# A state space layer scanned over 128 chunk states of four tokens instead of over 512 tokens

## The reference, cut to what matters

```python
bu_re = jnp.einsum('blgh,gph->blgp', uf, bbar_re)     # and bu_im
a_re = jnp.broadcast_to(ar, (1, L, SSM_GROUPS, SSM_STATE))   # ar, ai: the same at every token
_, _, xr, xi = lax.associative_scan(_s5_combine, (a_re, a_im, bu_re, bu_im), axis=1)
y = (jnp.einsum('blgp,ghp->blgh', xr, c_re) - jnp.einsum('blgp,ghp->blgh', xi, c_im) + d * uf)
y = jax.nn.gelu(y)
z = y @ w_glu + b_glu                                  # gated output of the mixer
```

## Time and profile before

| | |
|---|---|
| median of three runs | 2510.85 us (2506.82 to 2512.15) |
| the profiled execution | 2511.58 us, its span 2509.8 us |
| TensorE matmul busy | 2283.3 us (91% of the span) |
| VectorE busy | 1359.9 us (54%) |
| mean granted TensorE clock | 0.95 |
| last chunk of the mixer taken by VectorE (L1526) | starts at 249.98 us of the span |

### The profile page before, as it was taken

One profiled execution on the slowest core, in us unless ns is written; L12 is line 12 of the kernel. 1 busy time (PEld: TensorE's weight loads), 2 busy tenths in 40 slices (PEclk: granted clock), 3 DMA queues, 4 the chain that ended last, 5 costly groups with the idle time before them and its releaser, 6 DMA issues.

```text
span 2509.8 us, 28343 instructions
## 1 busy us (share of the span) xinstructions
PE 2283.3 (91%) x10166; PEld 1763.3 (70%) x10166; DVE 1359.9 (54%) x1988; ACT 924.8 (37%) x1334; POOL 263.4 (10%) x217
## 2 busy tenths in 40 slices
PE   5777888999998899999998789999979978999997
PEld 3511556788886688888887658888857865888885
DVE  7998555544445556665655454234258874532433
ACT  5400332322222555655554143123144432422322
POOL 4477003000004000000000100000100001000000
PEclk9898888999999999999999899999999988999999
DMA  3000011222322212212221212222211111222221
GB/s 147 32 0 0 26 67 67 84 92 92 103 79 103 86 66 81 80 63 80 69 74 55 68 67 91 93 101 100 77 50 68 58 51 67 100 87 98 101 91 43
DMA packets 32218, 185.50 MB, mean 74 GB/s; under 512 B 4753, under 2 KB 5009, under 8 KB 13457
## 3 DMA queue, kind: packets, MB, share of 16 engines
q1 hardware_dynamic: 27216, 176.17, 20.0%
q10 hardware_dynamic: 2880, 6.20, 0.7%
q0 software_dynamic: 2048, 2.17, 0.4%
HBM read 180.26 MB, written 2.10 MB: 73 GB/s over the span
## 4 chain that ended last, share of the span: by engine, by line
PE 74%; DVE 10%; issue 5%; ACT 5%; DVEq 4%; POOL 3%; ACTq 0%; DMA 0%; POOLq 0%
PE ps L516 14%; PE ps L518 14%; PE ps L517 14%; PE ps L833 5%; PE ps L835 5%; PE ps L834 5%; POOL prod L456 2%; PE ps L573 2%; PE ps L539 1%; PE ps L541 1%; PE ps L540 1%; DVE f_run L1937 1%; PE ps L652 1%; DVE rstd L1358 1%; ACT h L1253 1%
## 5 line engine op out<-in xcount | busy, mean ns | idle before, releaser
L516 PE MATMUL ps<-x_hi,w_lo 128*128 128x512 f32 x1024 | 403.6, 394 | 24.0 <-DVE u L1513 12.0
L517 PE MATMUL ps<-x_lo,w_hi 128*128 128x512 f32 x1024 | 401.9, 392 | 0.0
L518 PE MATMUL ps<-x_hi,w_hi 128*128 128x512 f32 x1024 | 401.7, 392 | 0.0
L970 ACT ACTIVATE w_hi<-raw 128x2048 fp32r<-128x2048 f32 x122 | 233.0, 1910 | 423.4 <-PE ps L518 362.7
L1346 DVE TENSOR_TENSOR w_lo<-raw,w_hi 128x2048 fp32r<-128x2048 f32 x122 | 284.5, 2332 | 97.0 <-ACT w_hi L970 96.7
L516 PEld LDWEIGHTS ps<-x_hi,w_lo 128*128 128x128 f32 x1024 | 194.5, 190 | 70.0 <-DVE w_lo L1346 25.1
L516 PE MATMUL ps<-hid_hi,w_lo 128*128 128x512 f32 x602 | 234.2, 389 | 0.0
L517 PE MATMUL ps<-hid_lo,w_hi 128*128 128x512 f32 x602 | 234.2, 389 | 0.0
L518 PE MATMUL ps<-hid_hi,w_hi 128*128 128x512 f32 x602 | 234.2, 389 | 0.0
L833 PE MATMUL ps<-x_hi,w_lo 128*128 128x512 f32 x560 | 229.1, 409 | 4.8 <-DVE w_lo L1819 4.8
L518 PEld LDWEIGHTS ps<-x_hi,w_hi 128*128 128x128 f32 x1024 | 194.2, 190 | 40.9
(11 more groups left out here) (344 smaller groups left out, 3619.2 us busy)
## 6 DMA issues: line engine op xcount, KB each, us to landing
raw<-w_attn_in SPq DMA_DIRECT2D x32, 1024.0 KB, 4.8
raw<-w_gate_up SPq DMA_DIRECT2D x22, 1024.0 KB, 4.8
raw<-w_up_a SPq DMA_DIRECT2D x16, 1024.0 KB, 4.8
raw<-w_down_a SPq DMA_DIRECT2D x16, 1024.0 KB, 4.8
raw<-w_up_h SPq DMA_DIRECT2D x16, 1024.0 KB, 4.8
raw<-w_down_h SPq DMA_DIRECT2D x16, 1024.0 KB, 4.8
raw<-w_hgrn_in SPq DMA_DIRECT2D x8, 1024.0 KB, 4.7
raw<-w_down SPq DMA_DIRECT2D x8, 768.0 KB, 4.2
```

Source lines behind the costliest of these rows:

```text
L516: pe.matmul(o, w_lo[:, slot, a:a + P], hi[:, k, :], start=k == 0, stop=False)
L517: pe.matmul(o, w_hi[:, slot, a:a + P], lo[:, k, :], start=False, stop=False)
L518: last = pe.matmul(o, w_hi[:, slot, a:a + P], hi[:, k, :], start=False, stop=k == st.kc - 1)
L970: act.activation(w_hi[:, slot, :], raw[:, slot, :], ACT.Copy).then_inc(whi_ready, 1)
```

## The change

With four tokens to a chunk (`STEP`), the state need only be known at the chunk's start. What the tokens of a chunk do to each other goes through a direct matrix of 128x128 for each of the distances 0 to 3 (`k_tau`), and what they add to the state at the chunk's end is summed by TensorE over the four phases (`ssm_in` with `lw`, which holds B times a power of a). Turning and scanning then run over 128 chunk states (`CHUNKS`) for each pair, in two batches of eight pairs, and the output of a token is C times a power of a (`ca_re`, `ca_im`) times the state before its chunk. u is stored by phase (`by_phase`), so that each phase's 128 tokens are contiguous.

New or altered on each engine: VectorE does the reciprocal and the first two tiles before the angles, does the angles of all pairs in seven 128x2048 instructions, and builds powers of a, `ab_re`/`ab_neg` and `ca_re`/`ca_im`. TensorE makes 32 transposes in place of 8 and 128 matmuls of 32x32 for `k_tau`, after the third slab. ScalarE copies eight banks to `lw` and four blocks to `k_tau`, and makes sine and cosine in three 128x2048 instructions. GpSimd only clears buffers. The turning back moves from GpSimd to VectorE. One of ScalarE's start DMAs is gone (B and C come compact in `bc_in`, C also padded as before), and `iota_in` is a quarter of its size.

```diff
+STEP = 4
+CHUNKS = T // STEP
+BATCHES = 2
...
-            for pr in range(N_PAIR):
-                for n, (part, by) in enumerate(((0, cos_t), (0, sin_t), (1, sin_t), (1, cos_t))):
-                    pool.wait_ge(scan_ready, 2 * pr + part + 1)
-                    if pr:
-                        pool.wait_ge(yssm_done, 4 * pr + n - 3)
-                    pool.tensor_tensor(prod[:, n, :], scan[pr % 2][part], by[:, pr, :], ALU.mult).then_inc(prod_ready, 1)
+            for pads in (ab_re, ab_neg, ca_re, ca_im):
+                last = pool.memset(pads[:, :, :, :], 0.0)
+            last.then_inc(pads_zero, 1)
...
+            def input_weights():
+                pe.wait_ge(ab_ready, 1)
+                for j in range(STEP):
+                    for n, ab in enumerate((ab_re, ab_neg)):
+                        if j:
+                            pe.wait_ge(lw_ready, 2 * j + n - 1)
+                        for i in range(4):
+                            last = pe.transpose(ps[:, 2 + n, i * P:(i + 1) * P], ab[:, j, 4 * i:4 * i + 4, :].rearrange("p a c -> p (a c)"), ident)
+                        last.then_inc(lw_done, 1)
+                for i in range(4):
+                    for tau in range(STEP):
+                        for ab, cc in ((ab_re, c_re), (ab_neg, c_im)):
+                            for q in range(4):
+                                at_ = GW * (STEP * i + tau)
+                                last = pe.matmul(ps[GW * q:GW * q + GW, 6, at_:at_ + GW], ab[:, tau, 4 * i + q, :],
+                                                 cc[:, 4 * i + q, :], start=cc is c_re, stop=cc is c_im)
+                last.then_inc(kt_done, 1)
...
+            def ssm_in(bt):
+                if bt:
+                    pe.wait_ge(bu_free, bt)
+                for ii in range(2):
+                    i = 2 * bt + ii
+                    for n in range(2):
+                        for l in range(STEP):
+                            for q in range(4):
+                                rows, at_ = slice(GW * q, GW * q + GW), 2 * P * n + P * ii
+                                last = pe.matmul(ps[:, 2 + q, at_:at_ + P], lw[rows, n, l, i, :], u[rows, i, l, :],
+                                                 start=l == 0, stop=l == STEP - 1)
                 last.then_inc(bu_done, 1)
...
+            def ssm_out(i):
+                for l in range(STEP):
+                    for ca, v in ((ca_re, v_re), (ca_im, v_im)):
+                        for q in range(4):
+                            last = pe.matmul(ps[GW * q:GW * q + GW, (6, SUM)[i % 2], P * l + 1:P * l + P],
+                                             ca[:, l, 4 * i + q, :], v[:, 4 * i + q, 0:CHUNKS - 1], start=False,
+                                             stop=l == STEP - 1 and ca is ca_im, skip_group_check=True)
+                last.then_inc(yssm_done, 1)
...
+            pe.wait_ge(ca_ready, 1)
+            for bt in range(BATCHES):
+                pe.wait_ge(v_ready, bt + 1)
+                for ii in range(2):
+                    if bt:
+                        ssm_direct(2 * bt + ii)
+                    ssm_out(2 * bt + ii)
...
+            def take(t):
+                dve.wait_ge(tile_done, t + 1)
...
             for c in range(5):
-                if c:
-                    split_lo(st, c, 0)
...
                 if c == 1:
+                    split_lo(st, 1, 0)
+                take(2 * c)
+                take(2 * c + 1)
+                if c in (1, 2, 3):
+                    split_lo(st, c + 1, 0)
+                if c == 0:
+                    angles()
+                if c == 1:
+                    input_powers()
                     input_matrix()
...
+                if c == 3:
+                    output_matrix()
...
             modulate(0)
...
+            demodulate(0)
+            modulate(1)
+            demodulate(1)
+            ssm_chunk(0)
+            ssm_chunk(1)
```

More of the change, by code:

```diff
@@ L593, in _ @@
                 if c == 2:
[L594 to L608 removed]
+                    input_weights()
@@ L609, in ssm_in, with ssm_direct @@
                 last.then_inc(bu_done, 1)
-            def ssm_out(pr):
-                i, q = divmod(pr, 4)
-                if q == 0 and i >= 2:
+            def ssm_direct(i):
+                if i >= 2:
                     pe.wait_ge(pre_gelu, i - 1)
-                for n, cc in enumerate((c_re, c_im, c_neg, c_im)):
-                    pe.wait_ge(prod_ready, 4 * pr + n + 1)
-                    pe.matmul(ps[GW * q:GW * q + GW, (6, SUM)[i % 2], :], cc[:, pr, :], prod[:, n, :],
-                              start=n == 0, stop=n == 3).then_inc(yssm_done, 1)
@@ L620, in _ @@
-            pe.wait_ge(blhs_ready, 1)
+                for tau in range(STEP):
+                    pe.matmul(ps[:, (6, SUM)[i % 2], P * tau:T], k_tau[:, i, tau, :],
+                              u[:, i, 0:STEP - tau, :].rearrange("p l c -> p (l c)"), start=tau == 0, stop=False,
+                              skip_group_check=True)
+            def ssm_out(i):
[6 more added lines that the diff above has]
+                last.then_inc(yssm_done, 1)
@@ L621, in _ @@
+            pe.wait_ge(lw_ready, 2 * STEP)
             pe.wait_ge(tile_free["dve"], STAGES["w_in"].tiles)
             ssm_in(0)
+            pe.wait_ge(kt_ready, 1)
+            pe.wait_ge(root_ready, SK["pre_mix"] + 1)
+            ssm_direct(0)
+            ssm_direct(1)
             ssm_in(1)
-            for pr in range(N_PAIR):
-                if pr + 2 < N_PAIR:
-                    ssm_in(pr + 2)
-                ssm_out(pr)
+            pe.wait_ge(ca_ready, 1)
[5 more added lines that the diff above has]
+                    ssm_out(2 * bt + ii)
@@ new lines, in by_power, with each_power, input_matrix @@
+            def by_power(table):
+                return table.unsqueeze(3).to_broadcast([P, STEP, N_PAIR, 16])
+            def each_power(n):
+                return bc[:, n, :, :].unsqueeze(1).to_broadcast([P, STEP, N_PAIR, 16])
+            def input_matrix():
+                g_re, g_im = by_power(gin[:, 0]), by_power(gin[:, 1])
+                for n, (by, src) in enumerate(((g_re, 2), (g_im, 3), (g_re, 3), (g_im, 2))):
+                    tt(ab_part[:, n], by, each_power(src), ALU.mult)
+                settle()
+                dve.wait_ge(pads_zero, 1)
+                for g in range(2):
+                    rows, cols = slice(64 * g, 64 * g + 64), slice(16 * g, 16 * g + 16)
+                    tt(ab_re[rows, :, :, cols], ab_part[rows, 0], ab_part[rows, 1], ALU.subtract)
+                    last = stt(ab_neg[rows, :, :, cols], ab_part[rows, 2], -1.0, ab_part[rows, 3], ALU.mult, ALU.subtract)
+                settle()
+                dve.sem_inc(ab_ready, 1)
@@ new lines, in angles @@
+            def angles():
+                steps = iota[:, :].unsqueeze(1).to_broadcast([P, N_PAIR, CHUNKS])
+                r_hi, r_lo, r_turn = (col(n).unsqueeze(2).to_broadcast([P, N_PAIR, CHUNKS]) for n in ("r_hi", "r_lo", "r_turn"))
+                ang, k, low = sin_c[:, :, :], cos_c[:, :, :], ang_low[:, :, :]
+                tt(k, steps, r_turn, ALU.mult)
+                tt(ang, steps, r_hi, ALU.mult)
+                settle()
+                ts(k, k, ROUND, None, ALU.add)
+                tt(low, steps, r_lo, ALU.mult)
+                settle()
+                stt(k, k, ROUND, ang, ALU.subtract, ALU.subtract)
+                settle()
+                tt(ang, low, k, ALU.subtract)
+                settle()
+                ts(ang, ang, 0.5, -0.5, ALU.min, ALU.max).then_inc(angle_ready, 1)
+                settle()
```

300 lines of the change are left out of this document (158 added, 142 removed).

## The result

The changed kernel takes 2432.0 us, the median of four runs (2428.5 to 2436.4), where the kernel before takes 2511.5. The ratio is 0.9688, with a 95% interval of 0.9667 to 0.9709. The profiled execution took 2430.4 us.

What follows compares the result with a forecast made beforehand. TensorE bounds the whole, but VectorE's scan, GpSimd's products and TensorE's reading bound the mixer loop. Terms summed to the last chunk ending at 197.3 instead of 249.98 us, saving 52.7: 2511.58 to 2458.9, forecast 2459, range 2440 to 2490.

Steps and rivals of the forecast that it cites:

- to the start of `ssm_in`: After TensorE's fourth slab: rounding 1.9, VectorE's rest 2.2, `output_matrix` 9.2 and the last two tiles 1.3 us.
- tail: End of the mixer: two `ssm_direct` 4.2 us, two `ssm_out` 13.7 us, and 2.5 us for the clock.
- I count nothing for that: GpSimd's work shrinks to five clearings, freeing VectorE of slow instructions; no gain was included in the sum.
- I take the serial 0.107: 13.7 us: Two `ssm_out` of 64 passes in the tail: no overlap on four column groups, 0.107 us a pass, 13.7 us.
- I take 0.05: 256 32-column `k_tau` passes at 0.05 us each, 12.8 us (ends 7 and 28); the same price for `ssm_in`, 6.4 us.
- Both signs by which the prediction was to show itself wrong first: `k_tau` passes taking 0.1 us or more, or a 1024-column VectorE instruction taking 2 us.
- The tail's direct products: Two `ssm_direct` on the path at the mixer's end, 4.2 us, plus 2.5 us for the clock after TensorE's idling.
- After the last chunk nothing of the program changes: Code behind the mixer's last chunk is unchanged, so the gain equals how much sooner that chunk ends: 52.7 us.
- The first, everything small overlaps: `k_tau` and `ssm_in` at 0.025 us a pass, `ssm_out` at 2.38 times: 17.5 us less, 2441 us; chance 0.15.
- The second (half clock, no overlap): TensorE's short bursts stay at half clock; `k_tau` and `ssm_in` at 0.107 us, tail doubled: 2494 us; chance 0.10.
- The third: VectorE's instructions with 16-element runs and tiles taken in steps of four tokens cost double: 21.6 us more, 2481; chance 0.13.
- The fourth: Slower than before: each pass pays load and stream in turn at half clock, 0.213 us; 2550 us; chance 0.04.

Runs made afterwards that it cites:

- the run by groups: The changed kernel with the column group as outermost loop of `ssm_out`, so 16 passes in a row go to the same 32 output rows; one run took 2437.4 us.
- the run with sixteen filling products: The changed kernel with sixteen unread 512-column products on TensorE before its wait for the second batch's turned states; the profiled execution took 2427.68 us.

## Why the prediction was wrong

The walk, with my marks and those of the profile after:

| step | forecast, us | measured, us | difference |
|---|---|---|---|
| input's matrices ready | at 78.9 | at 78.6 | -0.3 |
| transposes and copies | 7.0 | 6.3 | -0.7 |
| `k_tau`, 256 passes | 12.8 | 5.0 | -7.8 |
| fourth slab | 11.0 | 12.3 | +1.3 |
| to the start of `ssm_in` | 14.8 | 15.6 | +0.8 |
| first `ssm_in` | 8.9 | 6.4 | -2.5 |
| VectorE's two batches and a chunk | 40.75 | 40.4 | -0.4 |
| tail | 20.4 | 11.6 | -8.8 |
| hand-offs | 2.7 | in the rows above | -2.7 |

Together 21.1 us, which is 197.3 less 176.2.

**What was right.** The bound and its place: the mixer's stretch was set by VectorE and by products on GpSimd, and the change is worth the distance of the last chunk. VectorE's work behind `ssm_in` came out within 0.4 us over 40, and the angles at 14.0 us (42.33 to 56.35) where 13.8 had been forecast. The chunks, which write with a step of 16 bytes, take 1.12 us instead of 0.75. A scan of 128 columns takes 0.40 us and starts each 0.32, where I had 0.37. The fourth slab is longer because it did not find the clock that I gave it: from 89 to 104 us it was 0.89.

**What came out right by luck.** The matrices were ready within 0.3 us of the forecast by errors that cancel. The takes cost 2.0 to 2.1 us a pair and not 1.3, and `input_matrix` 9.9 us and not 9.2; against that the takes began at 40.3 us instead of 42.2 and `input_powers` took 5.9 instead of 6.7. When the same kernel is run again, the takes begin at 42.4 us and the matrices are ready at 80.7. One term was put at nothing ("I count nothing for that"): GpSimd's absence beside VectorE. The seven instructions that end with this one make the rotary angles in both kernels, and took from 33.5 to 39.7 us with GpSimd's angles beside them, which began at 33.8, and from 32.7 to 36.7 us without. Their last, before and now:

```profile
38.39 1.36 DVE L1445 TENSOR_SCALAR tmp<-tmp 128x512 f32<-128x512 f32 x1
36.35 0.43 DVE L1466 TENSOR_SCALAR tmp<-tmp 128x512 f32<-128x512 f32 x1
```

No run removes GpSimd's work alone. The reciprocal started at 36.7 us and not at 39.2; in other executions it waited for ScalarE's root until 38.1.

**What failed: the price of a narrow pass.** Two terms carry it. "I take the serial 0.107: 13.7 us" for `ssm_out` was wrong by a factor of three: 4.5 us, 0.030 a pass at full clock, and the run by groups shows that the order over the column groups makes the difference (0.092 in the other order). I had refused it because the only rows that showed an overlap were for row groups. "I take 0.05" for `k_tau` stood between ends of 7 and 28 us and should have been below the lower one: 5.0 with its pause, 2.9 without. I took 0.05 from passes of 128 columns, four times as wide, and counted width for nothing. `ssm_in` had the same 0.05 and took 0.030 at full clock; with the start at the low clock it came to 6.4 us. Both signs by which the prediction was to show itself wrong first (0.1 us a pass for `k_tau`, 2 us for a 1024-column instruction) are on the slow side, and neither came.

The Trainium skill (TensorE: Matmul & The Clock Gate, Part 3) speaks of column tiles as of row tiles and gives 2.38 times for three column tiles. The runs agree that they overlap: 0.030 us a pass on four column groups as on four row groups, 3.05 times faster than group by group on columns and 2.46 times on rows. Part 1 of the same page, with 62 ns for each small MATMUL with hardware decoding off, does not fit here: the 128 products, 256 passes, took 5.0 us, which is 39 ns a product and 20 ns a pass even with the pause counted. Which way decoding is set here no run shows.

**The tail's direct products** were forecast at 4.2 us and 2.5 for the clock, 6.7 together, and measured 4.61 + 2.35 = 7.0. That part held, and the run with sixteen filling products shows that the clock term was right in kind: 2.2 us of it vanish when TensorE hardly idles.

**What no term had.** By 21.1 us the sum would have given 2458.9 - 21.1 = 2437.8 us; the profiled execution took 2430.4. The other 7.4 us lie in the attention behind, unchanged code, which took 111.5 instead of 118.7 us with the granted clock at 0.88 instead of 0.81. "After the last chunk nothing of the program changes" is true of the program and was taken for true of the time. Its size could not have been read from the rows, since kernels with the changed mixer have anything from 8 us less to 1 us more than the kernel before.

**The rivals.** The first, everything small overlaps, is the one that came: it gives a last chunk at 197.3 - 17.5 = 179.8 us, 3.6 late, and 2441 us. It had 0.15, and the forecast, with both prices higher, 0.58. The second (half clock, no overlap) was right in that bursts behind an idle time start at the low level (0.50), but in the program's own order only for their first few us. Its price of 0.107 for `ssm_in` was that of the full clock; group by group at 0.50 a pass took 0.136. The third doubled the 16-element runs, and they cost nothing: 1.22 us for 1024 columns as before; only the takes' step cost something. The fourth had 0.213 us a pass, and 0.030 and less came.

## What to carry to other kernels

Before pricing many narrow matmuls, look at which row or column group each one uses compared with the one before it: in turn over four groups they cost a third (column groups) or four tenths (row groups) of what the same passes cost group by group, 0.030 us against 0.09 and 0.07 for 128 columns, so the order of the innermost loop is worth more than the count. Put work of an engine that others don't wait for yet (here 14 us of angles, half a matrix of coefficients, direct products) behind what they do wait for, and check that it removes an idle stretch of TensorE, since the first burst behind one can pay for the clock as well. And treat 7 us in unchanged code behind the change, out of 2430, as something that a change may shift either way: compare stretches with the granted clock beside them before giving it a cause.

## What the runs showed of the hardware that I had not expected

- Passes of 32 rows by 128 columns (on row groups) and of 128 rows into 32 output rows by 127 columns (on column groups) both go at 0.030 us each over four groups in turn. Group by group it is 0.074 (9.47 us for 128) and 0.092 (5.86 us for 64). These are at full clock.
- TensorE can be busy without a break and stay at the low clock: 128 passes of 32 rows, one row group at a time, had 0.50 granted for all of their 17 us.
- Products of 32 by 32 go at 0.011 us each in turn, with one pause of 1.8 to 2.5 us behind the 158th of 256 in eleven of eleven executions; group by group at 0.031 without it. What the pause is stays open.
- A step of 16 bytes in VectorE's SBUF operand makes a 512-column instruction 1.07 us instead of 0.68; in its PSUM operand it costs nothing.
- The granted clock over an unchanged stretch of 110 to 120 us differed from 0.80 to 0.91 between kernels, and by 0.01 with 2.9 us between two runs of the same one.
